# Row swaps of a rotary embedding: transfers inside SBUF issued by GpSimd in place of products with a swap matrix

## The reference, cut to what matters

```python
def apply_rope(x, cos, sin):            # block one: pairs of neighbouring features
    x1, x2 = x[..., 0::2], x[..., 1::2]
    y1 = x1 * cos - x2 * sin
    y2 = x1 * sin + x2 * cos
    return jnp.stack([y1, y2], axis=-1).reshape(x.shape)

def apply_rope_2(x, cos, sin):          # block two: the last 32 of 96 features, in halves of 16
    x1, x2 = jnp.split(x, 2, axis=-1)
    return jnp.concatenate([x1 * cos - x2 * sin, x2 * cos + x1 * sin], axis=-1)

q = apply_rope(rms_norm(q, q_g), cos, sin); k = apply_rope(rms_norm(k, k_g), cos, sin)   # x stream
q = concat([q[..., :64], apply_rope_2(q[..., 64:], cos2, sin2)])                         # block two
k_rope (32 features, shared by all heads) goes through apply_rope_2 as well
```

## Time and profile before

| | |
|---|---|
| median of three runs | 1647.05 us |
| the profiled execution's own time | 1644.55 us |
| its span in the trace | 1642.8 us |
| TensorE busy | 97% of the span |
| VectorE busy | 69% |
| ScalarE busy | 56% |
| GpSimd busy | 8% |
| data moved | 303.36 MB, mean 185 GB/s |

### The profile page before, as it was taken

One profiled execution on the slowest core, in us unless ns is written; L12 is line 12 of the kernel. 1 busy time (PEld: TensorE's weight loads), 2 busy tenths in 40 slices (PEclk: granted clock), 3 DMA queues, 4 the chain that ended last, 5 costly groups with the idle time before them and its releaser, 6 DMA issues. The chain is left out here.

```text
span 1642.8 us, 31046 instructions
## 1 busy us (share of the span) xinstructions
PE 1589.0 (97%) x12874; PEld 1463.2 (89%) x12874; DVE 1129.8 (69%) x1763; ACT 919.0 (56%) x1459; POOL 127.2 (8%) x106
## 2 busy tenths in 40 slices
PE   6999999999999999999999999999999999999999
PEld 3987478999999999966899999878999998799999
DVE  2799677645566655897765556778887567788873
ACT  3444756545365444647554446767666467676662
POOL 0230000112001100300011000000101000001110
PEclk9999999999999999999999999999999999999999
DMA  9443666656546555435566653323555533245553
GB/s 395 160 152 131 258 236 227 235 216 240 192 167 221 205 188 201 155 125 207 195 228 237 220 184 119 118 78 130 207 191 202 204 112 116 77 137 200 207 193 118
DMA packets 46172, 303.36 MB, mean 185 GB/s; under 512 B 5072, under 2 KB 7376, under 8 KB 12752
## 3 DMA queue, kind: packets, MB, share of 16 engines
q1 hardware_dynamic: 45312, 299.78, 50.7%
q0 software_dynamic: 288, 0.92, 0.1%
q10 hardware_dynamic: 432, 0.68, 0.1%
HBM read 298.22 MB, written 3.15 MB: 183 GB/s over the span
## 5 line engine op out<-in xcount | busy, mean ns | idle before, releaser
L2002 DVE TENSOR_TENSOR wl<-raw,wh 128x1040 fp32r<-128x1040 f32 (+1 forms) x472 | 576.4, 1260 | 295.8 <-ACT wh L1759 229.9
L1759 ACT ACTIVATE wh<-raw 128x1040 fp32r<-128x1040 f32 (+1 forms) x472 | 466.5, 1031 | 195.5 <-PE bank L1552 109.3
L1547 PE MATMUL bank<-hx_hi,wh 128*128 128x256 f32 x1856 | 519.6, 280 | 6.0 <-ACT hx_hi L1759 3.8
L1552 PE MATMUL bank<-hx_lo,wh 128*128 128x256 f32 x1856 | 516.2, 278 | 0.0
L1550 PE MATMUL bank<-hx_hi,wl 128*128 128x256 f32 x1856 | 514.7, 277 | 0.3 <-DVE wl L2002 0.2
L1547 PEld LDWEIGHTS bank<-hx_hi,wh 128*128 128x128 f32 x1856 | 349.0, 188 | 10.8 <-issue 9.8
L1550 PEld LDWEIGHTS bank<-hx_hi,wl 128*128 128x128 f32 x1856 | 349.1, 188 | 2.8 <-issue 1.7
L1552 PEld LDWEIGHTS bank<-hx_lo,wh 128*128 128x128 f32 x1856 | 348.8, 188 | 1.0 <-DVE hx_lo L1995 0.4
L1550 PE MATMUL bank<-hid_hi,wl 128*128 128x256 f32 x912 | 252.2, 277 | 1.4 <-DVE wl L2002 1.4
L1547 PE MATMUL bank<-hid_hi,wh 128*128 128x256 f32 x912 | 252.5, 277 | 0.3 <-ACT wh L1759 0.2
L1552 PE MATMUL bank<-hid_lo,wh 128*128 128x256 f32 x912 | 251.9, 276 | 0.0
(11 more groups left out here) (218 smaller groups left out, 1891.5 us busy)
## 6 DMA issues: line engine op xcount, KB each, us to landing
raw<-in_wts SPq DMA_DIRECT2D x208, 1032.0 KB, 4.9
raw<-in_wts SPq DMA_DIRECT2D x50, 1024.0 KB, 6.6
raw<-in_wts SPq DMA_DIRECT2D x20, 776.0 KB, 4.3
raw<-in_wts SPq DMA_DIRECT2D x4, 584.0 KB, 4.4
tscr<-tmp SPq DMA_DIRECT2D x4, 512.0 KB, 7.4
bias<-tscr SPq DMA_DIRECT2D x4, 512.0 KB, 6.0
raw<-in_wts SPq DMA_DIRECT2D x2, 648.0 KB, 4.0
xTc<-in_ctxT SPq DMA_DIRECT2D x1, 1024.0 KB, 10.6
```

Of the source, the lines that this page charges most:

```text
L1547: pe.matmul(out, block(f, M.wh, w0 + k, ncols, c, m), x_hi, start=first and k == 0 and o == 0, stop=False, skip_group_check=True)
L1552: ins = pe.matmul(out, block(f, M.wh, w0 + k, ncols, c, m), x_lo, start=False, stop=last and k == nk - 1, skip_group_check=True)
L1759: return act.activation(out, in_, func, bias=bias, scale=scale)
L2002: tt(M.wl[k][:, cols], M.raw[r][:, cols], M.wh[k][:, cols].bitcast(F32), ALU.subtract).then_inc(*on.inc(lo))
```

## The change

The swap matrices and their products go. Right after `hn1` a new step `swap` is put into the list for GpSimd alone: it waits for `xg` and for the target tile to be free, and issues two transfers from SBUF to SBUF, one for each direction of the swap, each with its own count on a semaphore of this swap. VectorE waits for both in place of the product. The sign that stood in the swap matrix now stands in the sine table (block one) and in the frequencies (block two). The tile `y` is taken at `hn1` and not at `hn2`; the banks `r` and `br`, the tile `y1` and the clearing of rows go. In block one VectorE's four instructions keep their order, with an operand from SBUF in place of the bank. In block two the cosine product now comes first and writes `q2` directly, and only the sine product and the addition, on the 32 rotated rows, wait for the transfers.

```diff
+PAIRS = ((slice(0, P, 2), slice(1, P, 2)), (slice(1, P, 2), slice(0, P, 2)))
+HALVES = ((slice(64, 80), slice(80, 96)), (slice(80, 96), slice(64, 80)))
...
+    def turned_rows(rows, src, dst, ready, free):
+        t = [ev(f"swap{n_turn[0]}", 16) for _ in range(2)]
+        n_turn[0] += 1
+        step("swap", rows=rows, src=src, dst=dst, ready=ready, free=free, t=t)
+        return t[-1]
...  heads_norm, right after the step hn1
+        if swap:
+            y = tmps.get()
+            t_r = turned_rows(PAIRS, xg.t[:, :], y.t, t_xg, y.free)
...  lora_norm, right after the step lora1
+            t_sw = turned_rows(HALVES, xg.t[:, 0:T], xg.t[:, T:2 * T], k_g, [])
...  latent_norm, right after the step hn1
+            y = tmps.get()
+            t_r = turned_rows(HALVES, xg.t[:, :], y.t, t_xg, y.free)
...  TensorE: hn2, qn2, lora2
-            mm(r.t[0:np_, :], swap, xg.t[0:np_, :], True, True).then_inc(*on.inc(t_r))
-        mm(r.t[0:96, :], M.swap2[0:96, 0:96], xg.t[0:96, :], True, True).then_inc(*on.inc(t_r))
-        mm(br.t[0:96, 0:T], M.swap2[0:96, 0:96], xg.t[0:96, 0:T], True, True).then_inc(*on.inc(t_sw))
...  VectorE, hn2
-        on.wait_ge(t_r, t_tab, y_free)
-        tt(v(y.t), v(r.t), wide(S), ALU.mult).then_inc(*on.inc(t_d[0]))
+        on.wait_ge(t_r, t_tab)
+        tt(v(y.t), v(y.t), wide(S), ALU.mult).then_inc(*on.inc(t_d[0]))
...  VectorE, qn2
-        on.wait_ge(t_r, t_tab, y_free)
-        tt(v(y.t), v(r.t), wide(M.ropeS), ALU.mult).then_inc(*on.inc(t_d[0]))
-        tt(v(xg.t), v(xg.t), wide(M.ropeC), ALU.mult).then_inc(*on.inc(t_d[1]))
-        on.wait_ge(t_d[1], out_free)
-        tt(M.q2[:, 2 * u:2 * u + 2, :], v(y.t), v(xg.t), ALU.add).then_inc(*on.inc(t_d[2]))
+        on.wait_ge(t_xg, t_tab, out_free)
+        tt(o, v(xg.t), wide(M.ropeC), ALU.mult).then_inc(*on.inc(t_d[0]))
+        on.wait_ge(t_r)
+        tt(v(y.t, 64), v(y.t, 64), wide(M.ropeS, 64), ALU.mult).then_inc(*on.inc(t_d[1]))
+        on.wait_ge(t_d[1])
+        tt(o[64:96, :, :], o[64:96, :, :], v(y.t, 64), ALU.add).then_inc(*on.inc(t_d[2]))
...  GpSimd
-    def lora1(xg, xg_free, z, **_):
-        on.wait_ge(xg_free)
-        pool.memset(xg.t[0:64, 0:T], 0.0).then_inc(*on.inc(z))
+    def swap(rows, src, dst, ready, free, t):
+        on.wait_ge(ready, free)
+        for (to, frm), t_i in zip(rows, t):
+            pool.dma_start(dst[to, :], src[frm, :]).then_inc(*on.inc(t_i, 16))
```

More of the change, by code:

```diff
@@ L80, in shape_constants @@
     c["bones"] = bo
[L81 to L91, removed]
+    sq = np.concatenate([c[k] for k in ("ident", "ones", "bones")], axis=1)
     t = np.arange(T)
@@ L632, in heads_norm @@
         banks.give(b, t_xg)
+        if swap:
+            y = tmps.get()
+            t_r = turned_rows(PAIRS, xg.t[:, :], y.t, t_xg, y.free)
         def rest():
             s, t_s = banks.get(), ev("mm")
-            r, t_r = (None, None) if swap is None else (banks.get(), ev("mm"))
-            s_free, r_free = s.free, r and r.free
+            s_free = s.free
             tmps.give(sq, t_s)
@@ L641, in rest @@
             banks.give(s, t_ln)
[L642 to L652, removed]
+            t_d = [ev("rope") for _ in range(4 if swap else 1)]
+            step("hn2", s=s, s_free=s_free, sq=sq, t_sq=t_sq, xg=xg, t_xg=t_xg, rs=rs, rs_free=rs_free,
+                 y=y if swap else None, blk=blk, tables=tables, nfeat=nfeat, np_=np_, out=out, out_free=out_free, t_s=t_s,
+                 t_r=t_r if swap else None, t_ln=t_ln, t_rs=t_rs, t_d=t_d)
+            tmps.give(xg, t_d[2 if swap else 0], t_r if swap else None)
+            if swap:
                 tmps.give(y, t_d[-1])
@@ L1303, in latent_norm @@
             banks.give(b, t_xg)
+            y = tmps.get()
+            t_r = turned_rows(HALVES, xg.t[:, :], y.t, t_xg, y.free)
             def rest():
-                s_, r, y = banks.get(), banks.get(), tmps.get()
-                t_s, t_r, t_ln, t_rs, t_d = ev("mm"), ev("mm"), ev("ln"), ev("rs"), [ev("rope") for _ in range(3)]
-                step("qn2", u=u, s=s_, s_free=s_.free, r=r, r_free=r.free, sq=sq, t_sq=t_sq, xg=xg, t_xg=t_xg, y=y,
-                     y_free=y.free, t_tab=list(t_rope), out_free=flat([rf, qs_free]), t_s=t_s, t_r=t_r, t_ln=t_ln,
-                     t_rs=t_rs, t_d=t_d)
+                s_ = banks.get()
+                t_s, t_ln, t_rs, t_d = ev("mm"), ev("ln"), ev("rs"), [ev("rope") for _ in range(3)]
+                step("qn2", u=u, s=s_, s_free=s_.free, sq=sq, t_sq=t_sq, xg=xg, t_xg=t_xg, y=y, t_tab=list(t_rope),
+                     out_free=flat([rf, qs_free]), t_s=t_s, t_r=t_r, t_ln=t_ln, t_rs=t_rs, t_d=t_d)
                 tmps.give(sq, t_s)
                 banks.give(s_, t_ln)
-                banks.give(r, t_d[0])
-                tmps.give(xg, t_d[2])
+                tmps.give(xg, t_d[1], t_r)
                 tmps.give(y, t_d[2])
```

69 lines of the change are left out of this document (32 added, 37 removed).

## The result

The changed kernel takes 1650.57 us in the median of 20 runs (1647.70 to 1652.68), the kernel before 1647.45 in 20 runs beside it (1646.03 to 1649.31). The ratio is 1.0017, 95% interval 1.0010 to 1.0023: slower by 3 us, where 1644.4 was forecast. The profiled execution took 1649.42 us.

The account below looks back on a forecast made before the run. TensorE was taken to bound the run only where it arrives last, with VectorE as full or fuller around block one's swaps. Terms -1.9 + 4.7 - 5.5 = -2.7 us gave 1644.4 on the 1647.05 median, range 1636 to 1652 (forecast's own 1641 to 1649).

Parts of the forecast that it names:

- TensorE alone deciding: Rival, whole kernel: TensorE's queue alone sets the time, up to 15.8 us faster, 1631 to 1638.5; chance 0.22.
- The transfers' cost: All 36 swap transfers: 0.54 us of GpSimd per issue, 2.3 us landing, rows ready 2.8 us after GpSimd starts.
- slower rival: Swaps in both blocks land late, as one store's 6.9 us: +10.1 us, 1657; slower from about 5.2 us; chance 0.20.
- At least 10 us of cover: Block one, first layer: swaps of k0, q1 and k1 meet an empty GpSimd and this much cover.
- the lock on descriptors: Rival: GpSimd's issue waits beside busy VectorE, at most 0.6 us per swap, 2.5 by the skill's figure; chance 0.05.
- Block one, second layer: q0's swap queues behind GpSimd's pooling branch, VectorE stalls 4.7 us, all reaching the end: +4.7 (-3.7 to +9.3).
- Edits at no cost: Both blocks: sine product reading SBUF instead of a bank takes the same 0.68 us; clears, constants and banks worth nothing.
- Block one, first layer: No stall at q0, 1.2 us to spare; the products of q1 and k1 gain: -1.9 us (-3.7 to 0).
- their 1.86 us turn into a longer wait there: Block one, first layer: products of q0 and k0 gain nothing, as VectorE's full queue sets the wait at 136.00.
- the step that kept the 1.86 us of q1 and k1: Block one, first layer: their products come at and after the wait at 136.00, so 1.86 us are kept.
- Block two: Each layer: no stall, TensorE gains 2.75 us of 4.19; two layers -5.5 us (-8.4 to 0).
- the six instructions of both follow the attention weights of 1083.8 directly: Block two, Q3 and Q2 on VectorE: done at 1086.4, so keys end at 1087.8 in place of 1090.51.

Follow-up runs that it names:

- no_swap: The changed kernel with neither transfers nor products, sine products reading xg itself (rotated half left out of the result): 1645.48 us, ratio 0.9983.
- split_pool: The changed kernel with GpSimd's pooling branch in block one's second layer cut in two around q0's swap: 1646.65 us, ratio 0.9995.
- pool_later: The changed kernel with GpSimd's part of the pooling branch behind q0's swap in block one's second layer: 1651.33 us, ratio 1.0023.
- dummy1: The changed kernel with TensorE making block one's eight 128x512 products again, unread: 1650.39 us, ratio 1.0020.
- free_sine: The changed kernel with VectorE's order sine, cosine, addition in block two, without the wait for the exponentials: 1648.09 us, ratio 1.0008.
- after: First profile of the changed kernel itself, against the kernel before: profiled execution 1649.42 us; median 1650.57 us, ratio 1.0017.
- again: The changed kernel once more, unaltered, for a second profile against the kernel before: 1649.78 us, ratio 1.0017.

## Why the prediction was wrong, step by step

- **What bounds the kernel** was read right: the products were worth little, since VectorE is the last to arrive around the swaps. no_swap puts it in one number: 15.8 us off TensorE, 2 to 3 off the time. TensorE alone deciding (1631 to 1638.5) is refuted by it.
- **The transfers' cost** was right in the median: 0.53 us of issue and 1.9 us to land, against 0.54 and 2.3. The slower rival's condition did occur, four of the 36 transfers landed after 5.1 to 7.2 us, over the 4 us that I had called a sign of being wrong; but these four, of k0 and q1, had the cover, and where the landing decided it took 2.3 to 2.7 us. (q0's second transfer in the first layer took 3.6 us and landed just as VectorE came to it, so the 1.2 us to spare were used up.) So the rival did not set the time. "At least 10 us of cover" in the first layer was misread for k1: its scaled copy ends at 154.0 us in the kernel before and VectorE asks at 156.75, 2.75 us later and less than the 2.8 that a swap was to take; with a fall of the clock ahead of it it waited (the 1.02 us above). No issue took over 0.71 us beside VectorE, so the lock on descriptors that the Trainium skill (SBUF — State Buffer, "SBUF: two separate sides") states did not show.
- **Block one, second layer: right.** Forecast: the last pooling instruction ends at 694.09, stall 4.7, term +4.7. Measured: it ends at 695.20 in an execution that is 1.5 us late there (the 0.3 us faster that I allowed it included), stall 4.67, term +4.6 and +5.1 in two profiles. That the queue order is the cause is shown by split_pool. That GpSimd's branch also slows VectorE I did not see, though the trace before had it (four taps in 3.84 us in place of 1.67), and so "Edits at no cost" was wrong of the sine product wherever it runs beside the branch; pool_later shows both.
- **Block one, first layer: forecast -1.9, measured -0.8 and +1.4.** The step "their 1.86 us turn into a longer wait there" was right; the step that kept the 1.86 us of q1 and k1 missed the clock. TensorE's wait grew from 1.55 to between 1.9 and 3.6 us, and in 8 of the 11 profiles in which VectorE reads no product in block one, in none of the other 4, the clock fell behind it. That costs what the two products bring. The six with the fall whose code in this layer is the changed kernel's ended at +0.7 to +1.8, the two without at -0.8; the mean of these eight is +0.8, that of the four profiles with products +0.5 (0.0 to +1.6). So no gain of this layer can be seen. Near 209 it stood at 0.5 for 6.8 us in 10 of the 11 and in 2 of the 4, and 0.4 to 1.7 us are lost there. What brings a fall in one execution and not in the next stays open: after 3.63 us of idle time there was none once, after 1.94 there was one, and giving TensorE its products back (dummy1) did not prevent it.
- **Block two: forecast -2.75 per layer, measured -1.3 and 0.0.** This is the step that failed. The first step, 1.40 us ahead by the key features and Q0, is right within 0.2. The step "the six instructions of both follow the attention weights of 1083.8 directly: 1082.4 + 4.0 = 1086.4" is wrong in three ways. The section on the change says that the cosine product comes first and writes `q2`; its wait was left out of the sum: it takes the wait for the output along, behind the exponentials, 0.68 us ahead of two instructions that used to cover it. The chain of three has two waits inside and not one, 0.34 us for both chains. And the weights were 1.2 us ahead, not 1.4. Together 1.2 us: the keys release TensorE 1.5 us earlier and not 2.75. free_sine, which takes back the first and a third of the second, regains 0.6 us at the keys and 0.9 by the end of the layer.
- **The second layer of block two** lost the rest to the clock. TensorE was 2.9 us ahead in its queue (3.26 forecast) and 1.5 at the keys, so its wait grew from 1.16 to 2.46 us; the clock then stood at 0.5 for 3.4 us, or 6.8. What it costs is read from the shift of the products: 1.65 us in the first layer, of which 1.6 were taken back at two waits that the kernel before had behind it (0.6 and 1.0 us), and 3.1 in the second, of which again only 1.6 came back. No part of my forecast had the clock in it. The Trainium skill (TensorE: Matmul & The Clock Gate, "Part 1: The HAM clock gate") says that the clock is at its low level by default and that activity releases it; the two rows at 0.50 and 0.65 above agree, and it is the rule that I should have weighed.

By the rows of "after" and "again", with the caution on block one, the terms are +0.3 (first layer, mean), +4.9, -1.3 and +0.1, together +4.0 in two executions, against my -2.7 and the medians' +3.1: block two accounts for 4.3 us of the difference, the first layer of block one for 2.2.

## What to carry to other kernels

Work taken from an engine that is ahead buys a longer wait, and on TensorE a longer wait may be followed by a fall of the clock: before taking it off, read who is last at each wait behind it, and count what is left of the gain after a few us at 0.5. When an instruction is moved ahead in a chain, its waits move with it; write them beside it and ask what used to cover each. A transfer that replaces a product needs its place in the issuing queue chosen, and cover on the consumer: with both (block two alone, and VectorE's order mended) the idea is worth 4.5 us here, without them it costs 3. And an engine that issues transfers beside other work has that work to be looked at, too: GpSimd's branch slowed VectorE whether or not the swap stood ahead of it.

## What the runs showed of the hardware

- Beside GpSimd's elementwise instructions most of VectorE's with two operands in SBUF took 1.6 to 2.7 times as long (0.69 us became 1.10 to 1.45, eight taps 5.66 in place of 3.25, four 3.84 in place of 1.67, two 2.38 in place of 0.87), while the one with an operand in a bank kept its 0.68.
- The clock stood at 0.5 for 3.4, 6.8 or 10.2 us at a time behind TensorE's waits in the 15 profiles, half of it work lost. After 1.1 to 1.2 us of idle time ahead of that score product of block two it did not fall (7 cases), after 1.7 to 2.5 us it did in 18 of 21. The length of the wait alone does not decide it: after the waits of 1.6 us near 1140 and 1465 us it fell once in 30.
- A transfer of 128 KB inside SBUF over every second partition landed in 2.4 us in the median (1.9 to 7.2; the slow ones where the transfer engines were busy 0.78 to 0.85 of the time). Of those of block two, 32 KB over 16 partitions or less, most landed in 1.6 to 1.8 us, and in 3.6 to 3.7 where the engines were busy 0.67 to 0.69.
- A wait between two VectorE instructions costs 0.11 us (0.71 between starts in place of 0.60), even where it has long been met (free_sine, sine to cosine product).
